# A product-key expert layer: chosen rows gathered, or both expert tables streamed once and used densely

## What is computed

```
PEER_HEADS, PEER_NKEYS, PEER_TOPK = 8, 128, 16          # 128*128 = 16384 experts
q = (h @ w_query).reshape(t, 8, 2, 128)
s = einsum('thpc,hpnc->thpn', q, sub_keys)              # 2 x 128 key scores per head
v1, i1 = top_k(s[:, :, 0], 16); v2, i2 = top_k(s[:, :, 1], 16)
cand = v1[..., :, None] + v2[..., None, :]              # 256 sums
best, pos = top_k(cand, 16)
experts = i1[pos // 16] * 128 + i2[pos % 16]
gate = softmax(best)
act = gelu(einsum('thkd,td->thk', expert_u[experts], h))
out = einsum('thk,thkd->td', gate * act, expert_v[experts])
```

## Time and profile before

| | us |
|---|---|
| runs shown | 1367.41, 1369.69, 1555.32 |
| median | 1369.69 |
| span of the profiled execution | 1367.2 |
| median less that span (launch and end) | 2.5 |
| before the expert layer | 0 to 249 |
| head of it: tile 1's projection, first queries | 249 to 309 |
| gathers one after another | 309 to 941 |
| second block | 941 to 1367 |

### The profile page before, as it was taken

One profiled execution on the slowest core, in us unless ns is written; L12 is line 12 of the kernel. 1 busy time (PEld: TensorE's weight loads), 2 busy tenths in 40 slices (PEclk: granted clock), 3 DMA queues, 4 the chain that ended last, 5 costly groups with the idle time before them and its releaser, 6 DMA issues.

```text
span 1367.2 us, 16345 instructions
## 1 busy us (share of the span) xinstructions
PE 1162.8 (85%) x5986; PEld 716.0 (52%) x5986; DVE 713.7 (52%) x1850; ACT 392.0 (29%) x1094; POOL 286.6 (21%) x275
## 2 busy tenths in 40 slices
PE   6999998989999987778777777778999998867896
PEld 4887877874555532223222223325978875332342
DVE  2365532487677777767777666644752515311112
ACT  2203532223333333333233334222531423000011
POOL 0000000024444444444444434440030000000000
PEclk9999999999999999999999999999999998999999
DMA  9711237399999999999999999997521474999996
GB/s 392 302 62 62 93 116 315 147 406 395 421 421 421 422 420 421 422 421 399 422 422 422 421 419 399 421 422 313 196 94 63 185 292 177 427 424 424 425 388 257
DMA packets 60283, 446.79 MB, mean 327 GB/s; under 512 B 6704, under 2 KB 7088, under 8 KB 10160
## 3 DMA queue, kind: packets, MB, share of 16 engines
q0 software_dynamic: 36864, 268.45, 47.5%
q1 hardware_dynamic: 22912, 175.97, 31.8%
q10 hardware_dynamic: 432, 1.40, 0.3%
HBM read 444.74 MB, written 1.05 MB: 326 GB/s over the span
## 4 chain that ended last, share of the span: by engine, by line
PE 52%; DMA 34%; DVE 6%; ACT 4%; issue 2%; SPq 0%; POOL 0%; DVEq 0%; ACTq 0%
DMA arena<-uv_in,arena 26%; PE bank L2478 12%; PE bank L2344 9%; DMA wring<-moe_in 4%; PE bank L2575 4%; PE bank L2821 3%; PE bank L2441 3%; PE bank L2837 2%; DMA wring<-stream_in 2%; DVE arena L1809 2%; PE bank L2780 2%; DMA arena<-moe_in 2%; PE bank L2572 2%; PE bank L2807 2%; PE bank L637 1%
## 5 line engine op out<-in xcount | busy, mean ns | idle before, releaser
L2478 PE MATMUL bank<-arena 128*128 128x512 f32 x1024 | 474.1, 606 | 116.9 <-ACT arena L1069 116.9
L1809 DVE CUSTOM_DVE_ANT_0 arena<-arena 128x1024 f32<-128x1024 f32 x256 | 314.0, 1226 | 192.5 <-DMA arena<-uv_in,arena 191.5
L787 POOL DMA_INDIRECT arena<-uv_in,arena x256 | 272.0, 1063 | 650.1 <-PE bank L2478 365.7
L2478 PEld LDWEIGHTS bank<-arena 128*128 128x128 f32 x1024 | 186.6, 191 | 374.3 <-ACT arena L1069 192.7
L1061 ACT ACTIVATE arena<-arena 128x2 f32<-128x2 f32 x128 | 26.2, 205 | 410.0 <-DVE arena L1809 409.8
L2344 PE MATMUL bank<-wring,arena 128*128 128x256 f32 x608 | 134.1, 381 | 1.0 <-DVE arena L1384 1.0
L2344 PEld LDWEIGHTS bank<-wring,arena 128*128 128x128 f32 x608 | 115.2, 191 | 17.7 <-DVE arena L1384 1.1
L1069 ACT ACTIVATE arena<-const,arena 128x128 f32<-128x128 f32 x256 | 86.7, 385 | 0.0
L2441 PEld LDWEIGHTS bank<-arena,wring 128*128 128x128 f32 x384 | 57.0, 196 | 20.2 <-issue 15.3
L2821 PE MATMUL bank<-arena 128*32 128x512 f32 x288 | 59.7, 616 | 7.5 <-DMA arena<-moe_in 4.9
L2821 PE MATMUL bank<-wring,arena 128*32 128x512 f32 x288 | 59.7, 620 | 7.2 <-DMA wring<-moe_in 7.2
(11 more groups left out here) (458 smaller groups left out, 1318.5 us busy)
## 6 DMA issues: line engine op xcount, KB each, us to landing
wring<-stream_in SPq DMA_DIRECT2D x67, 1024.0 KB, 8.9
wring<-moe_in SPq DMA_DIRECT2D x14, 2048.0 KB, 17.9
arena<-moe_in SPq DMA_DIRECT2D x26, 1024.0 KB, 17.7
arena<-moe_in SPq DMA_DIRECT2D x12, 2048.0 KB, 18.7
wring<-moe_in SPq DMA_DIRECT2D x13, 1024.0 KB, 14.2
arena<-uv_in,arena POOLq DMA_INDIRECT x256, 12.8
arena<-moe_in SPq DMA_DIRECT2D x4, 512.0 KB, 10.7
wring<-moe_in SPq DMA_DIRECT2D x4, 512.0 KB, 11.2
```

What stands on the lines that cost most here:

```text
L787: pool.indirect_dma_start(G[:, j, :], None, uv_d, src).then_inc(gathered[j], 16)
L1809: v.tensor_tensor_reduce(out=junk, in0=G[:, j, 0:D], in1=h2[:, t, :], scale=1.0, scalar=0.0, op0=ALU.mult, op1=ALU.add, accum_out=dots[:, ...
L2478: ins = mm(bank[1 + 2 * tile + c][:, :], diag[:, j, :], G[:, j, D + c * 512:D + (c + 1) * 512], start=False, stop=False, skip_group_check= ...
```

## The change

The layer is computed densely: every expert's activation for every token, then a weight that is zero but for the chosen ones, then the product with all of v. Three phases take the place of the gathers.

- **U.** 128 blocks of 128 experts. SP loads the u halves of two blocks (a pair) as four DMAs, in runs of 1 KB; VectorE transposes a block in 32x32 squares (`turn_u`, 1024 elements per partition, two buffers); TensorE multiplies with the tokens, 8 matmul statements of 128x256 per block; ScalarE writes gelu of a pair into G. G is [experts of a block, 128 blocks, 256 tokens], 128 KB of every partition. The tokens are first spread to match the 32x32 transposes (`spread_h2`). Queries, key scores and selection pieces are laid between the blocks; part of `decode` goes to GpSimd; expert numbers are kept as two key numbers per slot.
- **W.** For each token TensorE multiplies two matrices that hold the slots' first keys (times the gate) and second keys as ones among zeros: one 128x128 matmul statement, whose result is that token's 128x128 weights. Batches of 4 tokens, 64 batches: VectorE 4 tensor_scalar of 128x128 (`keys_hot`), GpSimd a subtraction of 128x512, ScalarE Abs and Relu of 128x512, TensorE 4 statements, then VectorE multiplies G in place (`weigh`, 128x512), reading PSUM along its rows and G with a step of 256 elements, which is 1 KB, from one element to the next.
- **V.** 64 pairs of blocks of v, 1 MB each, a ring of five buffers; 16 statements of 128x256 per pair into four banks; the last four pairs run tile by tile in columns of 128.

The output projection of tile 1 moves ahead of modulation group 5. Eight chunks of the next stage's weights are loaded during V, and its masks after it. The weights' ring and the arena become one tensor.

```diff
+QUERY_AT = {1 + 3 * i: EARLY_QUERIES + i for i in range(N_STEPS - EARLY_QUERIES)}   # 4 early, 16 steps
+GATES_AT = (44, 96)
+SLOTS_AT = (48, 100)
+PIECES_FAST = 36
 # SP
+            def u_in(m):
+                i = block_of(2 * m)
+                for a in range(4):
+                    sp.dma_start(raw[m % 3][32 * a:32 * a + 32],
+                                 uv_d[i * P:(i + 2) * P, a * T:(a + 1) * T].rearrange("(g r) c -> r g c", r=32))
+            for m in range(3, PAIRS_U):
+                sp.wait_ge(ut_ready, 2 * (m - 3) + 2)
+                u_in(m)
+            for c in range(V_RING, PAIRS_U):
+                sp.wait_ge(uv_used, BLOCKS_U + c + 1 - V_RING)
+                v_in(c)
 # GpSimd
-                pool.indirect_dma_start(G[:, j, :], None, uv_d, src).then_inc(gathered[j], 16)
+            for b in range(N_BATCH):
+                if b >= 4:
+                    pool.wait_ge(w_built, b - 3)
+                nc.gpsimd.tensor_tensor(hot2[b % 4], bc(lane, 1, BATCH), bc(key2T[:, BATCH * b:BATCH * (b + 1)], 2, P),
+                                        ALU.subtract).then_inc(hot2_ready, 1)
 # ScalarE
-            nc.scalar.activation(diag[:, at + q, :], ident, ACT.Copy, scale=weight[:, at + q:at + q + 1])
+                nc.scalar.activation(G[:, i:i + 2, :].rearrange("p i t -> p (i t)"), bank[1 + m % 2][:, :], ACT.Gelu)
+                    nc.scalar.activation(hot2[b % 4], hot2[b % 4], ACT.Abs).then_inc(act_step, 1)
+                    nc.scalar.activation(hot2[(b - 1) % 4], hot2[(b - 1) % 4], ACT.Relu, bias=ones[:, 0:1], scale=-1.0)
 # VectorE
-                        v.tensor_tensor_reduce(out=junk, in0=G[:, j, 0:D], in1=h2[:, t, :], ...)
+            def turn_u(n):
+                m, b = n // 2, n % 2
+                dve.wait_ge(uv_here[RAW_HOME[m % 3]], u_landed(m))
+                if n >= 2:
+                    dve.wait_ge(uv_used, n - 1)
+                v.transpose(UT[b].rearrange("p c (g r) -> p g c r", g=4),
+                            raw[m % 3][:, 4 * b:4 * b + 4, :].rearrange("p g (c s) -> p g c s", c=8)).then_inc(ut_ready, 1)
+            for n in range(BLOCKS_U):
+                if n >= 2:
+                    turn_u(n)
+                advance(pieces, 3 if n < PIECES_FAST else 2)
+                if n in GATES_AT:
+                    gates_of(GATES_AT.index(n))
+            def keys_hot(b):
+                for q in range(BATCH):
+                    tok = slice(BATCH * b + q, BATCH * b + q + 1)
+                    ins = v.tensor_scalar(hot1[:, b % 2, q], lane, key1T[:, tok], gateT[:, tok], ALU.is_equal, ALU.mult)
+            def weigh(b):
+                dve.wait_ge(w_built, b + 1)
+                some = G[:, :, BATCH * b:BATCH * (b + 1)].rearrange("p i t -> p t i")
+                v.tensor_tensor(some, some, bank[W_BANK[b % 4]][:, :].rearrange("p (t i) -> p t i", t=BATCH), ALU.mult)
+            for b in range(N_BATCH):
+                weigh(b)
+                if b + 2 < N_BATCH:
+                    keys_hot(b + 2)
 # TensorE
-                        ins = mm(bank[1 + 2 * tile + c][:, :], diag[:, j, :],
-                                 G[:, j, D + c * 512:D + (c + 1) * 512], start=False, stop=False)
+            for n in range(BLOCKS_U):
+                m, b = n // 2, n % 2
+                ...
+                pe.wait_ge(ut_ready, n + 1)
+                for c in range(KD):
+                    ins = mm(bank[1 + m % 2][:, b * T:(b + 1) * T], UT[b][:, c, :], h2P[:, c, :],
+                             start=c == 0, stop=c == KD - 1)
+            for b in range(N_BATCH):
+                ...
+                for q in range(BATCH):
+                    ins = mm(bank[W_BANK[b % 4]][:, q * P:(q + 1) * P], hot2[b % 4][:, q], hot1[:, b % 2, q],
+                             start=True, stop=True)
+            pe.wait_ge(bank_taken, N_BATCH)
+            for c in range(PAIRS_U - V_TAIL):
+                pe.wait_ge(uv_here[c % V_RING], v_landed(c))
+                for b in range(2):
+                    ins = values(c, b, range(KD), slice(0, T))
+                ins.then_inc(uv_used, 1)
```

More of the change, by code:

```diff
@@ L55, with chunk_slot, chunk_turn @@
 WSLOTS = 8
+RING = WSLOTS * CHUNK
+EXTRA_SLOTS = {C_Q: 8, C_SK: 9}
+def chunk_slot(n):
+    if C_Q <= n < C_IN2:
+        return EXTRA_SLOTS[n] if n in EXTRA_SLOTS else n - C_SK - 1
+    return n % WSLOTS
+def chunk_turn(n):
+    return sum(chunk_slot(m) == chunk_slot(n) for m in range(n + 1))
 SM = {}
@@ new lines, in _ @@
+            for b in range(N_BATCH + 1):
+                if b < N_BATCH:
+                    act.wait_ge(hot2_ready, b + 1)
+                    steps[0] += 1
+                    nc.scalar.activation(hot2[b % 4], hot2[b % 4], ACT.Abs).then_inc(act_step, 1)
+                if b > 0:
+                    act.wait_ge(act_step, steps[0] - (b < N_BATCH))
+                    nc.scalar.activation(hot2[(b - 1) % 4], hot2[(b - 1) % 4], ACT.Relu, bias=ones[:, 0:1], scale=-1.0)\
+                      .then_inc(hot2_done, 1)
@@ L1648, in best_keys @@
                 t, h = unit // PH, unit % PH
[L1649 to L1650 removed]
+                dve.wait_ge(keys_out, unit + 1)
+                src = keyS[t][:, h]
                 for first in (True, False):
@@ new lines, in gates_of, with selection @@
+            def gates_of(t):
+                dve.wait_ge(exped, t + 1)
+                link(v.tensor_reduce(gsum, by_head(t), AX, ALU.add))
+                link(v.reciprocal(gsum, gsum))
+                v.tensor_tensor(by_head(t), by_head(t), bc(gsum, 2, TOPK), ALU.mult).then_inc(gates_ready, 1)
+            def selection():
+                for t in range(NT):
+                    for h in range(PH):
+                        yield from best_keys(t * PH + h)
+                        yield from choose(t * PH + h)
+                    yield from under_top(t)
@@ new lines, in advance @@
+            def advance(pieces, n):
+                for _ in itertools.islice(pieces, n):
+                    pass
+            add_mixed(0)
+            finish_all(normed(0))
+            add_mixed(1)
+            turn_u(0)
+            turn_u(1)
+            finish_all(normed(1))
+            modulation(5)
+            pieces = selection()
+            for n in range(BLOCKS_U):
[4 more added lines that the diff above has]
+                    gates_of(GATES_AT.index(n))
@@ L2473, in weighted_rows @@
[L2473 to L2483 removed]
+                if s >= 2:
+                    pe.wait_ge(keys_out, s - 1)
```

741 lines of the change are left out of this document (348 added, 393 removed).

## The result

The changed kernel takes 1819.63 us (1817.85 to 1823.24, four runs), the kernel before 1370.33 beside it. One of the four runs of the kernel before, at 1555.32, is in a slower state of the chip and is left out of the ratio, which is 1.330, 95% interval 1.327 to 1.332. The prediction was 1825, range 1778 to 1895.

What follows compares the result with a forecast made beforehand. Bound by TensorE, then gathers (632 us), TensorE again, lastly weights' DMA. 248.6 + 54 + 506 + 133 + 456 = 1397.6 against 941.2, +456.4; less 0.7, span 1822.9, plus 2.5 around it, 1825 us; range 1778 to 1895.

Steps and rivals of the forecast that it cites:

- The mechanism: U and V: TensorE's 2048 statements at 0.442 us, 905 us, replace a gather stretch of 632 us.
- Rival 4: U and V: statements at one instruction, 0.221 us, lose 452 us; time 1373, no change; chance 0.03.
- U and V: Two dense phases, TensorE alone on the path at 0.221 us per instruction: U 506 us, V 456 us.
- W: Weighing phase, VectorE longest: 64 batches of 2.05 us plus 2 to fill, 133 us, ends 99 and 160.
- the middle, 1.13: W: weighing 512 elements beside GpSimd's subtraction, taken between 0.69 and 1.57 us.
- 0.85 for four tensor_scalar: W: VectorE's four tensor_scalar per batch, priced from a row of 8 in 1.7 us.
- Rival 1: W: the long step doubles element time, weighing 1.67 us with contention; W 168 us, time 1860; chance 0.16.
- contention of 0.44: W: time GpSimd's subtraction adds to each weighing, 1.23 us becoming 1.67.
- Rival 2: W: Abs and Relu each need a table load, ScalarE bounds; W 251 us, time 1943; chance 0.04.
- Rival 3: U bound by 1 KB loads (640 us, time 1959) or slow transposes (790 at most, 2110); chance 0.07.
- Head and end: Before U, 54 us; after the last v matmul, 11.5 us replaces 12.2, a gain of 0.7.
- The spreads: Head: two spreads of h2, 64 instructions each at 0.061 us, 3.9 us each, 7.8 together.

Runs made afterwards that it cites:

- upper-half kernel: The changed kernel with all U and V statements reading the upper 16 bits of their 32-bit numbers as bfloat16; 1384.59 us.

## Why the prediction was right, and where its terms were not

**The mechanism was right.** The argument that carried it, 2048 statements of two instructions each against a stretch of 632 us, was borne out from both sides: at full price PE has no idle microsecond in U and V; with statements left out, or at half the instructions and about half the price of each, 420 to 435 us go. Rival 4 (not slower) named 0.233 us per statement as its point of decision. The changed kernel paid 0.431; the upper-half kernel, at one instruction per statement, came within 1.2% of the kernel before.

**U and V, 26 us too much.** The step was sized 0.221 per instruction from 7.07 us for 32. A merged row ends when its last matmul leaves the pipe, 0.38 us after its start, and not one step after. In the changed kernel VectorE's transposes, which follow TensorE, give the step clean:

```profile
700.13 1.25 DVE L1737 STREAM_TRANSPOSE big<-big 128x1024 f32<-128x1024 f32 x1 [2.21 <-PE bank L2575]
703.59 1.25 DVE L1737 STREAM_TRANSPOSE big<-big 128x1024 f32<-128x1024 f32 x1 [2.21 <-PE bank L2575]
```

3.46 us for 16 instructions, 0.216 each. Over the 3968 instructions of 256 columns the difference to 0.221 is some 21 of the 26 us. The same correction to 32 instructions, (7.07 - 0.38) / 31, gives 0.216 from the earlier trace rows: it was to be had before.

**W, 32 us too little: the step that failed** is "GpSimd is at its subtraction for about half of each batch, so I take the middle, 1.13" and, beside it, 0.85 for four tensor_scalar. Measured are 1.30 and 1.40 (89.8 / 64). They overlap a little, and a batch takes 2.53 us, from the first weighing's start at 794.3 to the last one's at 953.7, where 2.05 were forecast; that is 30 of the 32 us. The first weighing starts 4.8 us into the stretch and not 2, which is the rest. The weighing's excess is all step (0.675 contiguous, 1.297 here, the same with GpSimd quiet), not contention. The contention sits in the scalars: 1.10 without it, 1.83 with it. And the 0.85 was taken from a row of one operation per element (L1637); these have two, with two scalar operands, and take 1.10 undisturbed; no run parts the second operation from the second scalar. L1918, the one row of contention before, was rightly seen as a warning and laid on the wrong instruction: it has two inputs in SBUF and weigh has one, which would fit, but no run changes that alone.

**Rival 1** is what W turned out as in time (168 forecast, 165.5 measured), and its reason, the step, was the larger half of it; its own contention of 0.44 on the weighing stood in for the scalars' by chance. Its total of 1860 is 40 us too high all the same, and the forecast's own total stayed so near the measured one only because U, V, the head and the end were sized too large.

**Rival 2** is refuted: Abs and Relu alternate at 0.63 and 0.71 us with no table load between. **Rival 3** is refuted as a bound. Its worry about runs of 1 KB had ground, as these loads get 225 GB/s and not 421, but U would have been bound only below the 136 that it asks for. The transposes cost 1.245, what the 1024-element dot product costs, so the output scattered in runs of 32 adds nothing over that row; no run transposes into adjacent numbers.

**Head and end.** The spreads, sized from a row of 256 columns, are of 128 and take half, 1.95 each. From the last v matmul to the gates' products 9.2 us pass, not 11.5, with the sums between the projection's first matmuls; another 1.5 in the second block has no single place that I looked for.

**Left open**: what lowers TensorE's clock in W is seen only as a pattern, rests of up to 1.8 us between batches go with 0.68 and rests of 0.65 with 0.98. I made no run that changes the rests alone.

## What to carry to other kernels

Before trading bytes for arithmetic, multiply the statements by their step: here 134 MB less traffic was worth at most some 130 us, as TensorE stood right behind the gathers, and the dense form asked some 880 us of TensorE. Count instructions per statement in the trace, since for 32-bit operands there are two. Take a price from start to start, never from a merged row divided by its count. For an elementwise operation with a long step, ask how many adjacent numbers it takes before each jump: turning the loops so that four, 16 bytes, lie together halved it for nothing. And look at what else the engine meets once an operation is shorter: of the 40 us that this freed, half was taken back until GpSimd was out of the way too.

## What the runs showed of the hardware that I had not expected

- VectorE reads PSUM with a step of 512 bytes as fast as contiguous: 0.675 and 0.676 us for 512 elements.
- TensorE writes PSUM with a step of 16 bytes at no price: 1.16 us for eight instructions of 128 columns either way.
- Loads of 256 KB in runs of 1 KB, to 32 partitions each, fill the DMA engines at 225 GB/s; loads of 1 MB, nearly all in runs of 4 KB to 128 partitions, at 396.
- GpSimd's 128x512 subtraction stretches four tensor_scalar from 1.10 to 1.83 us and leaves a tensor_tensor with one input in PSUM as it was, 1.29 us beside it and 1.31 without.
- TensorE reads the upper halves of 32-bit numbers, a step of 4 bytes in both operands, in one instruction per statement and not two: a load of 128x128 in 0.097 us against 0.190 for 32 bits, and a step of 0.114 us for 256 columns against 0.216. No adjacent 16-bit numbers were run beside it.
